# A hybrid decoder block on one core: x and the first two weight units in 256 KB pieces, transposes one piece ahead, high passes first, positions later

## Chip, cores and metric

The kernel runs on one core of a Trainium2 chip. The time is device time of the whole program in microseconds (us), the median of several runs. The profile is of one execution, whose own time stands beside its span, from the first to the last instruction.

## The reference, cut to what matters

One decoder block on 256 tokens of width 1024, in float32. An input projection feeds two groups of heads (a gated linear attention and a block attention), their outputs go through an output projection, and a gated feed-forward network follows.

```python
h = rms_norm(x, norm1_gain[l])
proj = h @ w_in[l]                       # 1024 x 3600
gq, gk, gv, gr, g_low, mq, mk, mv = ...  # slices of proj
gate_logit = (g_low @ w_gate_up[l] + b_gate[l])
log_a = jax.nn.log_sigmoid(gate_logit) / GLA_GATE_TAU
# o_gla from gq, gk, gv, gr, log_a; o_moba from rotary(mq, positions), rotary(mk, positions), mv
x = x + jnp.concatenate([o_gla, o_moba], axis=-1) @ w_out[l]
h = rms_norm(x, norm2_gain[l])
x = x + (jax.nn.silu(h @ w_ffn_gate[l]) * (h @ w_ffn_up[l])) @ w_ffn_down[l]
return rms_norm(x, final_norm_gain)
```

## The kernel before, in words

**Products in three passes.** Every float32 product is made of three matmuls of a rounded type: high part of the activations by high part of the weights (line 433), high by low (434), low by high (435). So each weight is split before use: ScalarE copies `raw` to `w_hi` (`split`, line 782), VectorE subtracts to get `w_lo` (line 997). The activations of the first projection are x transposed, multiplied by the norm gain and split in the same way: ScalarE writes `aT_hi` (line 805), VectorE `aT_lo` (line 1001). The factor of the norm, one number per token (`rstd`), is put in when a result is taken out of PSUM.

**Units and buffers.** Weights come in units of 1 MB (2048 columns per partition): `w_in` is units 0 to 11, two units (row blocks 0 to 3 and 4 to 7) for each of six blocks of 512 columns. `raw` has three slots (`RAW`), `w_hi` and `w_lo` six (`RING`). A slot of `raw` is loaded again when the low part of the unit in it is made (`raw_free`). All loads of x and the weights are issued by the SyncE queue, in the order of the code: x as two tiles of 128 tokens (512 KB each, line 278), unit 0 in two halves (line 311), the narrow columns of the gate (`low_raw`, 64 KB in pieces of 64 bytes, line 313), units 1 and 2 (line 282), six small tensors, then unit 3 and on as slots come free. GpSimd issues two small loads of its own, positions and frequencies (lines 369 and 370), before it builds the identity matrix `ident` (371, 372) that the transposes need.

**The start.** TensorE waits for `ident`, transposes the gains (449), runs four warm-up transposes (455), transposes x, tile by tile, 16 transposes (462), runs eight more warm-up transposes and then `first_unit`: for each of four row blocks k it waits for `aT_hi`, `aT_lo`, `w_hi`, `w_lo` of that row block and issues its six matmuls. We call these six a row. Unit 0 is rows 0 to 3, unit 1 rows 4 to 7. Between them come `gate_low` (16 matmuls, lines 495 and 496, whose left operand is `low_w`, split by ScalarE at 821 and GpSimd at 407) and the transposes of the other gains (483). After unit 1 come the logits (529), then units 2 to 11, with small steps between or inside them: `cumulate` (538, 540) in the middle of unit 3 needs the logarithms of the gate from VectorE (1059); `moba_transposed(1)` (522) in the middle of unit 7 needs the second rotated operand from VectorE (1081).

**The queues of the other engines.** Each engine works strictly in the order written. VectorE: activations and weights of rows 0 to 3 in turn, activations 4 to 7, unit 1, the take-out of `gate_low` (1025) and of the gains (1027), units 2 and 3, the scaled logits (1034), the angles of the rotation with the end of the gate in the middle (1059), units 4 and 5, the gate's factors on queries and keys (1086 to 1091), units 6 and 7, the first rotation, unit 8, and so on. ScalarE: activations and weights in pairs, the narrow columns (821), unit 1, the sums of squares of x (788), units 2 and 3, the take-out of block 0 (799), the gate's functions (831 to 833), units 4 and 5, the exponentials of the cumulated gate (839 to 841, which wait for `cumulate`), unit 6, sine and cosine, unit 7, the take-out of block 1, and on. GpSimd: the two loads, `ident`, the masks, the low part of the narrow columns (407), `rstd` (402, 403).

Of the kernel before, what the change touches and what calls it, by code (L numbers as in the profile page):

```python
# [22 lines left out]
P = 128  # L23
SEQ, D = 256, 1024
T = SEQ // P
# [20 lines left out]
IN_UNITS, OUT_UNITS = 2 * len(BLOCKS), 4  # L46
PHASE0 = IN_UNITS + OUT_UNITS
# [29 lines left out]
def fill(u):  # L77

    return u // RAW + (1 if u % RAW else 0)


def build_block(nc, x, positions, norm1_gain, w_in, w_gate_up, b_gate, gla_out_gain, moba_out_gain,
# [6 lines left out]
    with ExitStack() as ctx:  # L89
# [18 lines left out]

        ident = sb("ident", [P])
# [73 lines left out]
        x_loaded = [sem(f"x_loaded_{t}") for t in range(T)]  # L183
# [4 lines left out]
        first_loaded = [sem(f"first_loaded_{n}") for n in range(2)]  # L188
# [87 lines left out]
        def _(sp):  # L276
            for t in range(T):
                sp.dma_start(x_sb[:, t, :], x[0, t * P:(t + 1) * P, :]).then_inc(x_loaded[t], 16)
# [35 lines left out]
            for u in range(1, RAW):  # L314
                rows_unit(u, w_in[0], (u % 2) * 4 * P, 4, BLOCKS[u // 2], 512)
# [43 lines left out]
        def _(pool):  # L359
# [40 lines left out]
            def wide_rstd(norm, t):  # L400
# [28 lines left out]
        def _(pe):  # L429
# [16 lines left out]

            pe.wait_ge(ident_built, 1)
# [4 lines left out]
            def warm_up(n):  # L452

                for _ in range(n):
# [830 lines left out]
```

## Time and profile before

| | us |
|---|---|
| median of 3 runs | 315.05 (314.77 to 315.11) |
| the profiled execution's own time | 314.29 |
| its span | 312.3 |
| start of the first matmul of a product | 9.66 |

The page is of that one execution; times in its rows count from the first instruction. Matmul and weight-load rows are modelled in their ends, so the distance between the starts of like instructions tells more than their durations. "TensorE's granted clock" is the column PEclk. In the mean it is 0.997 of full speed.

### The profile page before, as it was taken

The page shows a single profiled execution, that of the slowest core. Times are in us where ns is not written, and L with a number is a line of the kernel's source. Part 1 is how long each engine was busy: PE and PEld are TensorE (multiplying, and loading weights), DVE is VectorE, ACT ScalarE, POOL GpSimd, SP SyncE. Part 2 cuts the span into 40 slices and gives each one's busy share as a digit, 9 for nine tenths or more (in the row PEclk, how much of TensorE's full clock was granted, in tenths as well). Part 3 has the DMA queues.
Part 4 walks back from the last instruction along what each step waited for, and adds up shares of the span by engine and source line. Part 5 has one row for each costly group of instructions (what it writes and reads, how often), then busy time and mean ns, then how long its engine had stood idle before and what let it go on. Part 6 is the DMA issues. An engine that isn't in the chain of part 4 may idle for free.

```text
span 312.3 us, 3865 instructions
## 1 busy us (share of the span) xinstructions
PE 301.4 (97%) x1424; PEld 251.2 (80%) x1424; DVE 178.9 (57%) x199; ACT 153.7 (49%) x185; POOL 21.9 (7%) x44
## 2 busy tenths in 40 slices
PE   5899999999999999999999999999999999999992
PEld 5787888888888888888888888888888888888881
DVE  0888979986686247645371809082635536280434
ACT  2978897568553437361533526070807152443124
POOL 7130100000202001500000000000000000000002
PEclk9999999999999999999999999999999999999998
DMA  7986386537744303928374564729090918330003
GB/s 224 367 277 244 118 295 206 192 134 270 253 148 139 134 0 82 309 81 283 123 242 163 184 220 137 266 72 331 18 376 9 326 77 274 129 134 0 0 2 135
DMA packets 36449, 54.45 MB, mean 174 GB/s; under 512 B 2834, under 2 KB 25540, under 8 KB 36436
## 3 DMA queue, kind: packets, MB, share of 16 engines
q1 hardware_dynamic: 36356, 54.24, 51.1%
q0 software_dynamic: 64, 0.03, 0.3%
q8 instruction: 8, 0.13, 0.2%
q14 instruction: 5, 0.04, 0.0%
q10 hardware_dynamic: 16, 0.00, 0.0%
HBM read 53.23 MB, written 1.05 MB: 174 GB/s over the span
## 4 chain that ended last, share of the span: by engine, by line
PE 94%; DMA 2%; DVE 1%; ACT 1%; issue 0%; SPq 0%; POOLq 0%; POOL 0%; DVEq 0%
PE acc L433 16%; PE acc L435 15%; PE acc L434 15%; PE aux L435 13%; PE aux L433 13%; PE aux L434 13%; PE aux L522 4%; DMA raw<-in_w_in 2%; PE aux L600 1%; DVE x_sb L1188 1%; PE aux L622 1%; PE aux L582 1%; PE aux L568 1%; DVE reuse_e L1246 0%; ACT reuse_e L974 0%
## 5 line engine op out<-in xcount | busy, mean ns | idle before, releaser
L997 DVE TENSOR_TENSOR w_lo<-raw,w_hi 128x2048 fp32r<-128x2048 f32 x48 | 107.9, 2287 | 15.2 <-ACT w_hi L782 15.2
L782 ACT CAST w_hi<-raw 128x2048 fp32r<-128x2048 f32 x48 | 89.7, 1912 | 6.5 <-PE acc L435 4.6
L433 PE MATMUL aux<-w_hi,aT_hi 128*128 128x512 f32 x176 | 69.7, 396 | 0.0
L435 PE MATMUL aux<-w_hi,aT_lo 128*128 128x512 f32 x176 | 68.8, 391 | 0.0
L434 PE MATMUL aux<-w_lo,aT_hi 128*128 128x512 f32 x176 | 68.5, 389 | 0.0
L433 PE MATMUL acc<-w_hi,aT_hi 128*128 128x512 f32 x136 | 54.9, 403 | 1.1 <-DVE w_lo L1013 1.1
L435 PE MATMUL acc<-w_hi,aT_lo 128*128 128x512 f32 x136 | 53.1, 391 | 0.0
L434 PE MATMUL acc<-w_lo,aT_hi 128*128 128x512 f32 x136 | 53.0, 390 | 0.0
L1220 DVE TENSOR_TENSOR pT_lo<-aux,pT_hi 128x512 fp32r<-128x512 f32 x10 | 6.9, 692 | 70.6 <-ACT pT_hi L943 70.6
L943 ACT CAST pT_hi<-aux 128x512 fp32r<-128x512 f32 x10 | 5.9, 587 | 76.5 <-PE aux L522 76.5
L435 PEld LDWEIGHTS aux<-w_hi,aT_lo 128*128 128x128 f32 x176 | 33.0, 188 | 7.1
L434 PEld LDWEIGHTS aux<-w_lo,aT_hi 128*128 128x128 f32 x176 | 33.1, 188 | 6.6
L433 PEld LDWEIGHTS aux<-w_hi,aT_hi 128*128 128x128 f32 x176 | 33.0, 188 | 6.5
L433 PE MATMUL acc<-w_hi,pT_hi 128*128 128x512 f32 x80 | 31.2, 390 | 0.0
L435 PE MATMUL acc<-w_hi,pT_lo 128*128 128x512 f32 x80 | 31.1, 389 | 0.0
L434 PE MATMUL acc<-w_lo,pT_hi 128*128 128x512 f32 x80 | 31.1, 389 | 0.0
L433 PEld LDWEIGHTS acc<-w_hi,aT_hi 128*128 128x128 f32 x136 | 25.6, 188 | 6.6 <-issue 1.6
L435 PEld LDWEIGHTS acc<-w_hi,aT_lo 128*128 128x128 f32 x136 | 25.5, 188 | 5.5
L434 PEld LDWEIGHTS acc<-w_lo,aT_hi 128*128 128x128 f32 x136 | 25.6, 188 | 4.9
L930 ACT ACTIVATE reuse_c<-aux,rstd 128x256 f32<-128x256 f32 x22 | 10.4, 473 | 26.3 <-PE aux L435 26.2
L434 PEld LDWEIGHTS acc<-w_lo,pT_hi 128*128 128x128 f32 x80 | 15.0, 188 | 3.1
L435 PEld LDWEIGHTS acc<-w_hi,pT_lo 128*128 128x128 f32 x80 | 15.0, 188 | 3.1
(170 smaller groups left out, 237.4 us busy)
## 6 DMA issues: line engine op xcount, KB each, us to landing
raw<-in_w_in SPq DMA_DIRECT2D x24, 512.0 KB, 4.9
raw<-in_w_ffn_gate SPq DMA_DIRECT2D x22, 512.0 KB, 4.4
raw<-in_w_ffn_up SPq DMA_DIRECT2D x22, 512.0 KB, 5.5
raw<-in_w_ffn_down SPq DMA_DIRECT2D x22, 512.0 KB, 5.8
raw<-in_w_out SPq DMA_DIRECT2D x8, 512.0 KB, 4.0
x_sb<-in_x SPq DMA_DIRECT2D x2, 512.0 KB, 3.8
out<-reuse_e SPq DMA_DIRECT2D x4, 256.0 KB, 2.4
reuse_a<-in_final_norm_gain SPq DMA_DIRECT2D x1, 512.0 KB, 4.7
```

Of the source, the lines that this page charges most:

```text
L433: nc.tensor.matmul(dst, left_hi[:, k, tok], right_hi, start=first, stop=False)
L434: nc.tensor.matmul(dst, left_hi[:, k, tok], right_lo, start=False, stop=False)
L435: return nc.tensor.matmul(dst, left_lo[:, k, tok], right_hi, start=False, stop=last)
L522: last = nc.tensor.transpose(aux[:, bank, n * P:(n + 1) * P], src, ident[:, :])
L568: last = nc.tensor.matmul(aux[:, bank, pair * SEQ:(pair + 1) * SEQ], kiT[:, pair, tok], qdT[:, pair, :, tok], start=True, stop=True)
L582: last = nc.tensor.matmul(aux[:, 2 + h // 2, (h % 2) * SEQ:(h % 2 + 1) * SEQ], mT[:, 0, h, P:SEQ], mT[:, 1, h, :], start=True, stop=True)
L600: last = nc.tensor.matmul(aux[:, bank, h * DV:(h + 1) * DV], probT[:, t + k, h, :], mv[:, k, h * DV:(h + 1) * DV], start=k == 0, stop=k == t)
L782: nc.scalar.copy(w_hi[:, slot % RING, :], raw[:, slot % RAW, :]).then_inc(hi_ready, 1)
L930: nc.scalar.activation(silu_g[:, t, :], aux[:, GATE_UP_BANKS[parity][t], 0:FF], ACT.Silu, scale=rstd[:, 1, t:t + 1]).then_inc(silu_ready, 1)
L943: nc.scalar.copy(dst, aux[:, 1, :].rearrange("p (k s) -> p k s", k=2)).then_inc(hiddenT_hi_ready, 1)
L997: nc.vector.tensor_tensor(w_lo[:, slot % RING, :], raw[:, slot % RAW, :], w_hi[:, slot % RING, :].bitcast(f32), ALU.subtract).then_inc(lo_ ...
L1220: nc.vector.tensor_tensor(lo, aux[:, 1, :].rearrange("p (k s) -> p k s", k=2), hi.bitcast(f32), ALU.subtract).then_inc(hiddenT_lo_ready, 1)
```

## The change

It does the following.

- x is loaded in four pieces of 256 columns for all 256 tokens (256 KB, contiguous pieces of 1 KB) and units 0 and 1 in eight pieces of one row block (256 KB, pieces of 2 KB), in the order x0, w0, w1, x1, w2, w3, x2, w4, w5, x3, w6, w7. The narrow columns and unit 2 follow, then the small tensors.
- TensorE begins with seven ordinary float32 matmuls of 64 columns on a tile of zeros that VectorE sets at its start, does the gains, seven more, then the four transposes of x piece 0, two more warm-up matmuls, row 0, and so on, the transposes of a piece one piece ahead of the rows. Rows 0 to 6 come before `gate_low` and the other gains, row 7 and the logits after.
- Within a row the order is both high by high matmuls, both high by low, both low by high, with a wait ahead of each pair for just what it needs.
- The high part of weight row 0 is made by VectorE; ScalarE makes those of rows 1 to 7, in an order of weights, weights, activations. VectorE subtracts in the same order. Units are counted from 2 in the semaphores of the splits.
- GpSimd issues the loads of positions and frequencies after the low part of the narrow columns.

```diff
-            for t in range(T):
-                sp.dma_start(x_sb[:, t, :], x[0, t * P:(t + 1) * P, :]).then_inc(x_loaded[t], 16)
+            def x_part(p):
+                cols = slice(p * 2 * P, (p + 1) * 2 * P)
+                sp.dma_start(x_sb[:, :, cols], x[0, :, cols].rearrange("(t p) n -> p t n", p=P)).then_inc(x_loaded[p], 16)
+
+            def first_part(n):
+                sp.dma_start(raw[:, n // 4, (n % 4) * 512:(n % 4 + 1) * 512],
+                             w_in[0, n * P:(n + 1) * P, BLOCKS[0]:BLOCKS[0] + 512]).then_inc(first_loaded[n], 16)
+
+            for p in range(X_PARTS):
+                x_part(p)
+                for n in (2 * p, 2 * p + 1):
+                    first_part(n)
...
             def raw_free(u):
 
-                if isinstance(u, int) and u == RAW:
-                    sp.wait_ge(first_lo_ready, 4)
+                if isinstance(u, int) and u < RAW + EARLY:
+                    sp.wait_ge(first_lo_ready, 4 * (u - RAW + 1))
                 else:
-                    sp.wait_ge(lo_ready, u - RAW)
-            buf = raw[:, 0, :].rearrange("p (k n) -> p k n", k=4)
-            for h in range(2):
-                sp.dma_start(buf[:, 2 * h:2 * h + 2, :], w_in[0, 2 * h * P:2 * (h + 1) * P, BLOCKS[0]:BLOCKS[0] + 512]
-                             .rearrange("(k p) n -> p k n", p=P)).then_inc(first_loaded[h], 16)
+                    sp.wait_ge(lo_ready, u - RAW - EARLY + 1)
+
             sp.dma_start(low_raw[:, :, :], w_in[0, :, LOW:LOW + RANK].rearrange("(k p) n -> p k n", p=P)).then_inc(low_loaded, 16)
-            for u in range(1, RAW):
+            for u in range(EARLY, RAW):
                 rows_unit(u, w_in[0], (u % 2) * 4 * P, 4, BLOCKS[u // 2], 512)
...
-            with nc.allow_non_contiguous_dma(reason="256 positions, one per partition and tile"):
-                pool.dma_start(pos_i[:, :], positions.rearrange("b (t p) -> p (b t)", p=P)).then_inc(pos_loaded, 16)
-            pool.dma_start(freq[:, :], inv_freq.to_broadcast([P, HALF])).then_inc(pos_loaded, 16)
             then(nc.gpsimd.memset(ident[:, :], 0.0))
             nc.gpsimd.affine_select(out=ident[:, :], in_=ident[:, :], compare_op=ALU.not_equal, fill=1.0, base=0,
                                     pattern=[[-1, P]], channel_multiplier=1).then_inc(ident_built, 1)
...
             pool.wait_ge(low_hi_ready, 1)
             nc.gpsimd.tensor_tensor(low_w[:, :, :, 1, :], low_raw[:, :, :].unsqueeze(2).to_broadcast(LOW_COPIES),
                                     low_w[:, :, :, 0, :].bitcast(f32), ALU.subtract).then_inc(low_lo_ready, 1)
+            with nc.allow_non_contiguous_dma(reason="256 positions, one per partition and tile"):
+                pool.dma_start(pos_i[:, :], positions.rearrange("b (t p) -> p (b t)", p=P)).then_inc(pos_loaded, 16)
+            pool.dma_start(freq[:, :], inv_freq.to_broadcast([P, HALF])).then_inc(pos_loaded, 16)
             for t in range(T):
                 wide_rstd(0, t)
...
-                pe.wait_ge(hi_ready, u)
-                pe.wait_ge(lo_ready, u)
+                pe.wait_ge(hi_ready, u - EARLY + 1)
+                pe.wait_ge(lo_ready, u - EARLY + 1)
...
+            def warm_up(n):
+
+                for _ in range(n):
+                    nc.tensor.matmul(acc[:, 2, 0:P // 2], warm[:, :], warm[:, 0:P // 2], start=True, stop=True)
+
+            pe.wait_ge(warm_built, 1)
+            warm_up(7)
             pe.wait_ge(ident_built, 1)
             pe.wait_ge(norm1_loaded, 16)
             nc.tensor.transpose(acc[:, 3, NORM1_ROW:NORM1_ROW + KC], gain_rows[0:KC, :],
                                 ident[0:KC, 0:KC]).then_inc(gains_in_psum, 1)
...
-            def warm_up(n):
-
-                for _ in range(n):
-                    nc.tensor.transpose(acc[:, 2, 0:P], ident[:, :], ident[:, :])
-
-            warm_up(4)
-            for t in range(T):
-                pe.wait_ge(x_loaded[t], 16)
-                for bank in range(4):
-                    for k in (2 * bank, 2 * bank + 1):
-                        last = nc.tensor.transpose(aux[:, bank, (k % 2) * SEQ + t * P:(k % 2) * SEQ + (t + 1) * P],
+            warm_up(7)
+
+            def x_transposed(part):
+
+                pe.wait_ge(x_loaded[part], 16)
+                for k in (2 * part, 2 * part + 1):
+                    for t in range(T):
+                        last = nc.tensor.transpose(aux[:, part, (k % 2) * SEQ + t * P:(k % 2) * SEQ + (t + 1) * P],
                                                    x_sb[:, t, k * P:(k + 1) * P], ident[:, :])
-                    if t == T - 1:
-                        last.then_inc(xT_in_psum, 1)
-
-            warm_up(8)
-
-            def first_unit():
-
-                for k in range(4):
-                    pe.wait_ge(xT_hi_ready, k + 1)
-                    pe.wait_ge(xT_lo_ready, k + 1)
-                    pe.wait_ge(first_hi_ready, k + 1)
-                    pe.wait_ge(first_lo_ready, k + 1)
-                    for t in range(T):
-                        last = product(acc[:, t, :], k, t, *weights(0, 512, k), k == 0, False)
-                last.then_inc(unit_used, 1)
+                last.then_inc(xT_in_psum, 1)
+
+            def first_row(k):
+
+                right_hi, right_lo = weights(k // 4, 512, k % 4)
+                toks = [slice(t * P, (t + 1) * P) for t in range(T)]
+                pe.wait_ge(xT_hi_ready, k + 1)
+                pe.wait_ge(first_hi_ready, k) if k else pe.wait_ge(row0_hi_ready, 1)
+                for t in range(T):
+                    nc.tensor.matmul(acc[:, t, :], aT_hi[:, k, toks[t]], right_hi, start=k == 0, stop=False)
+                pe.wait_ge(first_lo_ready, k + 1)
+                for t in range(T):
+                    nc.tensor.matmul(acc[:, t, :], aT_hi[:, k, toks[t]], right_lo, start=False, stop=False)
+                pe.wait_ge(xT_lo_ready, k + 1)
+                for t in range(T):
+                    last = nc.tensor.matmul(acc[:, t, :], aT_lo[:, k, toks[t]], right_hi, start=False, stop=k == KC - 1)
+                    if k == KC - 1 and t == 0:
+                        last.then_inc(tile0_in_psum, 1)
+                if k % 4 == 3:
+                    last.then_inc(unit_used, 1)
...
-                     7: [moba_scores], 9: [moba_outputs]}
-            for u in range(IN_UNITS):
-                if u == 0:
-                    first_unit()
-                else:
-                    in_unit(u, midway.get(u, ()))
+            after = {4: [gla_transposed], 6: [gla_scores], 7: [moba_scores], 9: [moba_outputs]}
+            x_transposed(0)
+            warm_up(2)
+            first_row(0)
+            x_transposed(1)
+            first_row(1)
+            x_transposed(2)
+            first_row(2)
+            first_row(3)
+            x_transposed(3)
+            for k in range(4, 7):
+                first_row(k)
+            gate_low()
+            other_gains()
+            first_row(7)
+            logits()
+            for u in range(EARLY, IN_UNITS):
+                in_unit(u, midway.get(u, ()))
                 for step in after.get(u, ()):
                     step()
...
+            def split_first(n):
+                act.wait_ge(first_loaded[n], 16)
+                cols = slice((n % 4) * 512, (n % 4 + 1) * 512)
+                nc.scalar.copy(w_hi[:, n // 4, cols], raw[:, n // 4, cols]).then_inc(first_hi_ready, 1)
 
 
             act.wait_ge(gains_ready, 1)
             take_xT((0, 1))
-            split_first(0)
-            take_xT((2, 3))
-            split_first(1)
-            take_xT((4, 5, 6, 7))
+            for p in range(1, X_PARTS):
+                split_first(2 * p - 1)
+                split_first(2 * p)
+                take_xT((2 * p, 2 * p + 1))
+            split_first(7)
             act.wait_ge(low_loaded, 16)
             nc.scalar.copy(low_w[:, :, :, 0, :], low_raw[:, :, :].unsqueeze(2).to_broadcast(LOW_COPIES)).then_inc(low_hi_ready, 1)
-            split(1)
+            split(2)
             for t in range(T):
-                act.wait_ge(x_loaded[t], 16)
                 sum_squares(0, t)
-            split(2)
             split(3)
             take_block(0, gqk)
...
-            def split_first(k):
-                dve.wait_ge(first_hi_ready, k + 1)
-                cols = slice(k * 512, (k + 1) * 512)
-                nc.vector.tensor_tensor(w_lo[:, 0, cols], raw[:, 0, cols], w_hi[:, 0, cols].bitcast(f32),
+            def split_first(n):
+                slot, cols = n // 4, slice((n % 4) * 512, (n % 4 + 1) * 512)
+                if n:
+                    dve.wait_ge(first_hi_ready, n)
+                else:
+                    dve.wait_ge(first_loaded[0], 16)
+                    nc.vector.tensor_copy(w_hi[:, 0, cols], raw[:, 0, cols]).then_inc(row0_hi_ready, 1)
+                    dve.wait_ge(row0_hi_ready, 1)
+                nc.vector.tensor_tensor(w_lo[:, slot, cols], raw[:, slot, cols], w_hi[:, slot, cols].bitcast(f32),
                                         ALU.subtract).then_inc(first_lo_ready, 1)
 
+            nc.vector.memset(warm[:, :], 0.0).then_inc(warm_built, 1)
             dve.wait_ge(gains_in_psum, 1)
             nc.vector.tensor_copy(gains[:, 0:KC], acc[:, 3, 0:KC]).then_inc(gains_ready, 1)
             dve.wait_ge(gains_ready, 1)
-            for k in range(4):
-                take_xT((k,))
-                split_first(k)
-            take_xT((4, 5, 6, 7))
-            split(1)
+            split_first(0)
+            take_xT((0, 1))
+            for p in range(1, X_PARTS):
+                split_first(2 * p - 1)
+                split_first(2 * p)
+                take_xT((2 * p, 2 * p + 1))
+            split_first(7)
             dve.wait_ge(low_in_psum, 1)
```

## Rows read from the trace of the kernel before

**Rows 1.** The page, part 1: busy us of each engine.

```profile
PE 301.4 (97%) x1424; PEld 251.2 (80%) x1424; DVE 178.9 (57%) x199; ACT 153.7 (49%) x185; POOL 21.9 (7%) x44
```

**Rows 2.** The chain that ended last, in order of time: start, us, what.

```profile
1.71 6.44 DMA raw<-in_w_in
...
24.22 0.43 PE acc L433
...
32.61 0.86 PE aux L538 x4
...
59.96 0.87 PE aux L522 x8
...
302.15 0.70 DVE x_sb L1188
```

**Rows 3.** Stretches: us, busy of each engine, granted clock, DMA share, GB/s.

```profile
5.50:6.50 1.00, 1.00 (x7) 1.00 (x6) 0.00 (x0) 0.00 (x0) 0.93 (x6) 1.00 0.93 185
10.00:11.00 1.00, 1.00 (x6) 0.83 (x5) 1.00 (x3) 1.00 (x4) 0.00 (x0) 1.00 1.04 383
```

**Rows 4.** GpSimd's queue, 4 to 8 us (packets, MB, share); landings of x, `in_w_ffn_gate`.

```profile
q0 software_dynamic: 63, 0.03, 20.1%
...
DMA to landing us min/median/max: 3.4/3.8/4.3
...
DMA to landing us min/median/max: 3.9/4.4/6.2
```

**Rows 5.** Timeline of GpSimd at the start: start, us, engine, line, operation.

```profile
1.32 0.93 POOL L369 DMA_DIRECT2D pos_i<-in_positions  x1 [0.82 <-POOLq L1275]
2.25 0.58 POOL L370 DMA_DIRECT2D freq<-in_inv_freq  x1
```

**Rows 6.** Timeline of TensorE, 3.6 to 17.4 us.

```profile
3.63 0.27 PE L449 MATMUL acc<-ident,reuse_d 8*128 8x8 f32 x1 [3.63 <-POOL ident L372]
...
5.59 0.63 PE L462 MATMUL aux<-ident,x_sb 128*128 128x128 f32 x2
...
7.02 0.49 PE L462 MATMUL aux<-ident,x_sb 128*128 128x128 f32 x3
...
9.66 0.47 PE L433 MATMUL acc<-w_hi,aT_hi 128*128 128x512 f32 x1 [1.06 <-DVE w_lo L1013]
...
15.19 0.28 PE L495 MATMUL acc<-aT_hi,w_hi 128*128 128x256 f32 x1
...
16.98 0.28 PE L496 MATMUL acc<-aT_lo,w_hi 128*128 128x256 f32 x1
```

**Rows 7.** Weight loads by line: count, ns min/median/max, starts.

```profile
L449 PEld LDWEIGHTS acc<-ident,reuse_d x1: 178/178/178, 3.6 to 3.6; 8*128 8x128 f32 x1
...
L483 PEld LDWEIGHTS acc<-ident,reuse_d x1: 132/132/132, 17.2 to 17.2; 10*128 10x128 f32 x1
...
L600 PEld LDWEIGHTS aux<-mv,reuse_f x24: 188/192/192, 78.1 to 80.7; 128*128 128x128 f32 x24
```

**Rows 8.** Timeline of ScalarE.

```profile
7.17 0.84 ACT L805 ACTIVATE aT_hi<-aux,gains 128x256 fp32r<-128x256 f32 x2 [4.47 <-PE aux L462]
8.17 1.14 ACT L811 CAST w_hi<-raw 128x512 fp32r<-128x512 f32 x2 [0.16 <-DMA raw<-in_w_in]
...
34.38 0.60 ACT L839 ACTIVATE reuse_c<-aux 128x512 f32<-128x512 f32 x1 [0.84 <-PE aux L540]
```

**Rows 9.** Timeline of VectorE.

```profile
17.30 0.41 DVE L1025 COPY lowT<-acc 32x256 f32<-32x256 f32 x1
...
18.88 4.49 DVE L997 TENSOR_TENSOR w_lo<-raw,w_hi 128x2048 fp32r<-128x2048 f32 x2 [1.09 <-ACT w_hi L782]
24.26 0.88 DVE L1034 SCALAR_TENSOR_TENSOR reuse_b<-aux,rstd,mv 128x256 f32<-128x256 f32 x2 [0.89 <-PE aux L529]
...
30.08 0.69 DVE L1059 SCALAR_TENSOR_TENSOR reuse_b<-reuse_b 128x512 f32<-128x512 f32 x1
...
58.46 0.69 DVE L1081 TENSOR_TENSOR reuse_e<-reuse_e,mv 128x512 f32<-128x512 f32 x1
```

More of the change, by code:

```diff
@@ L46 @@
 IN_UNITS, OUT_UNITS = 2 * len(BLOCKS), 4
+EARLY = 2
+X_PARTS = 4
 PHASE0 = IN_UNITS + OUT_UNITS
@@ L77, in fill @@
 def fill(u):
-    return u // RAW + (1 if u % RAW else 0)
+    return u // RAW + (1 if u % RAW >= EARLY else 0)
 def build_block(nc, x, positions, norm1_gain, w_in, w_gate_up, b_gate, gla_out_gain, moba_out_gain,
@@ L107, in build_block @@
         pT_lo = sb("pT_lo", [2, SEQ], f32r)
+        warm = sb("warm", [P])
         ident = sb("ident", [P])
@@ L180, in build_block @@
         ang, turns, turns_lo, sin_arg = (reuse_e[:, n * T * HALF:(n + 1) * T * HALF] for n in range(4))
-        x_loaded = [sem(f"x_loaded_{t}") for t in range(T)]
+        x_loaded = [sem(f"x_loaded_{p}") for p in range(X_PARTS)]
         rows_loaded = sem("rows_loaded")
@@ L187, in build_block @@
         bias_loaded = sem("bias_loaded")
-        first_loaded = [sem(f"first_loaded_{n}") for n in range(2)]
+        first_loaded = [sem(f"first_loaded_{n}") for n in range(4 * EARLY)]
+        warm_built = sem("warm_built")
+        row0_hi_ready = sem("row0_hi_ready")
         up_loaded = sem("up_loaded")
@@ L708, in _ @@
                       9: [probs_transposed], 10: [gla_updates], 11: [lambda: heads_transposed(0, (3, 0)), gla_outputs]}
-            after = {0: [gate_low, other_gains], 1: [logits], 4: [gla_transposed], 6: [gla_scores],
-                     7: [moba_scores], 9: [moba_outputs]}
-            for u in range(IN_UNITS):
-                if u == 0:
-                    first_unit()
-                else:
-                    in_unit(u, midway.get(u, ()))
+            after = {4: [gla_transposed], 6: [gla_scores], 7: [moba_scores], 9: [moba_outputs]}
[16 more added lines that the diff above has]
+                in_unit(u, midway.get(u, ()))
                 for step in after.get(u, ()):
@@ L806, in take_xT @@
                                   gains[:, NORM1_ROW + k:NORM1_ROW + k + 1]).then_inc(xT_hi_ready, 1)
-            def split_first(half):
-                act.wait_ge(first_loaded[half], 16)
-                for k in (2 * half, 2 * half + 1):
-                    nc.scalar.copy(w_hi[:, 0, k * 512:(k + 1) * 512], raw[:, 0, k * 512:(k + 1) * 512]).then_inc(first_hi_ready, 1)
+            def split_first(n):
+                act.wait_ge(first_loaded[n], 16)
+                cols = slice((n % 4) * 512, (n % 4 + 1) * 512)
+                nc.scalar.copy(w_hi[:, n // 4, cols], raw[:, n // 4, cols]).then_inc(first_hi_ready, 1)
             act.wait_ge(gains_ready, 1)
             take_xT((0, 1))
-            split_first(0)
-            take_xT((2, 3))
-            split_first(1)
-            take_xT((4, 5, 6, 7))
+            for p in range(1, X_PARTS):
[3 more added lines that the diff above has]
+            split_first(7)
             act.wait_ge(low_loaded, 16)
             nc.scalar.copy(low_w[:, :, :, 0, :], low_raw[:, :, :].unsqueeze(2).to_broadcast(LOW_COPIES)).then_inc(low_hi_ready, 1)
-            split(1)
+            split(2)
             for t in range(T):
-                act.wait_ge(x_loaded[t], 16)
                 sum_squares(0, t)
-            split(2)
             split(3)
@@ L951, in ffn_phase @@
                 for n in range(n_units):
-                    split_as(slot + 3 + n, fills - (0 if (slot + n) % RAW else 1), u + (n + 4 - RING))
+                    split_as(slot + 3 + n, fills + (1 if (slot + n) % RAW >= EARLY else 0), u + (n + 4 - RING))
                 take_gate(j, u, parity)
@@ L995, in split @@
                 slot = u if slot is None else slot
-                dve.wait_ge(hi_ready, u)
+                dve.wait_ge(hi_ready, u - EARLY + 1)
                 nc.vector.tensor_tensor(w_lo[:, slot % RING, :], raw[:, slot % RAW, :],
```

## The prediction

> **What bounds the kernel now.** First the page's busy times: TensorE works 301.4 of 312.3 us [rows 1], so the time is TensorE's order plus what lies before and after it. The chain that ended last says where it is not TensorE: it starts with the load of the first weights, landing at 1.71 + 6.44 = 8.15, reaches TensorE's products at 9.66 and leaves them at 302.15 [rows 2, 6]. Between these TensorE has no wait worth naming, so a gain at the start reaches the end only if every later wait has room for it. So the third reading is the timelines of the other engines: how much earlier could TensorE come to each step before its input is the late one? Two places are tight. `cumulate` starts at 32.61 and its input, from VectorE's line 1059, is ready at 30.08 + 0.69 = 30.77: room 1.84. `moba_transposed(1)` starts at 59.96, its input is ready at 58.46 + 0.69 = 59.15: room 0.81 [rows 2, 9].
>
> **The loads.** In 5.50 to 6.50 the DMA engines moved 185 GB/s, at 10 to 11 us 383 [rows 3]; GpSimd's two small loads took 20% of the engines' time in 4 to 8 us for 0.03 MB [rows 4]. Issued later, they leave that room to x and the weights. At 383 GB/s a 256 KB piece takes 0.68 us. The x tiles (pieces of 4 KB, 512 KB each) took 3.4 and 4.3 us from issue to landing; the quickest load in pieces of 1 KB, also 512 KB, 3.9 [rows 4]. Half of it is 0.7 less: x0, issued at 0.8, lands at about 4.0. One piece lands per 0.68 us after it: w0 4.7, x1 6.0, x2 8.1, x3 10.1, w7 11.5, with the narrow columns behind at 12.5 and unit 2 at 15. SyncE issues 12 loads in place of 4, at some 0.4 us each, quicker than they move. What waits on w0 to w7 and x0 to x3 is costed below; landings by this list come before each use.
>
> **The moved loads' other side.** GpSimd spends 0.93 + 0.58 issuing them [rows 5], now behind the low part of the narrow columns and ahead of `rstd`; both `rstd` and positions are then needed only after 24 us, some 3 and 1.5 us after I have them ready. `ident`, for which TensorE waited to 3.63 [rows 6], comes those 1.5 us earlier, at 2.1.
>
> **The warm-up.** VectorE's memset lets TensorE start at about 1.05. Seven float32 matmuls are 14 matmul instructions: an ordinary float32 matmul shows as two. What does one of 64 columns cost, with its weight load of 128 columns? The trace has none. Its bounds: the transposes of 128 columns are 0.21 apart at the start (two in 0.63, less the 0.42 of the last), so 64 columns are 0.107, nothing less; at most a slow weight load. A transpose's weight load takes 178 ns before the clock rises and 132 after [rows 7]: 46 ns that scale and 86 that don't. An ordinary one takes 188 at the quick clock, so 102 scale, and 204 ns at the slow one. I take 0.21, the nearer to these rows. At the quick clock it is 0.107 either way. TensorE's page in the Trainium skill, "TensorE: Matmul & The Clock Gate", LDWEIGHTS, gives columns by 1.2 GHz, 107 ns for 128 columns with no word on the clock gate; by it the warm-up would cost 1.5 us each time, which is the second case below. No row here shows it at the slow clock.
>
> When does the clock rise? PEclk says 1.00 from the first microsecond, but the starts tell otherwise: equal transposes stand 0.21 apart at 5.6 us and 0.11 (0.49 less 0.27, halved) at 7.0 [rows 6]; 1.2 and 2.4 GHz. The change of step lies at 6.7, 3.1 us after TensorE's first work at 3.63. I take the same after its new start, some 4.3. So: first seven 1.05 to 4.0; gains to 4.2; second seven, nearly all quick, to 5.8; the four transposes of x0, landed long since, 0.45 to 6.25; two warm-up matmuls to 6.7, in the shadow of ScalarE's first `aT_hi` (7.17 for two took 0.84 [rows 8], so 0.42 each: 6.35 to 6.8). The first weight row is ready by then (copy and subtract, 0.7 each, from 4.7). **Row 0 starts at S = 6.8 instead of 9.66.**
>
> **The rows.** 24 matmuls of unit 0 took 9.66 to 15.19, so a row is 1.38 [rows 6]. Does anyone keep TensorE waiting once it runs? ScalarE does two weight rows (0.57 each) and two activations (0.42) per pair, 2.0 us; VectorE some 0.65 for a weight row (a quarter of half of 4.49 [rows 9], and its fixed part) and as much as ScalarE for the activations, 2.2 us; TensorE's pair with its transposes takes 3.2. Walked through from S: row 0 has its last pair at S + 0.9, its `aT_lo` at S + 0.85; every later row finds its inputs 0.3 us or more early, with x1 and x2 landed. So the dense stretch begins at S. High passes first are what makes row 0 start on `w_hi` and `aT_hi` alone; if all four inputs had to be there it would cost 0.85.
>
> Before the take-out of `gate_low` there now stand seven rows, three groups of transposes and 16 matmuls (15.19 to 16.98 and the next, 1.9 [rows 6]): 9.7 + 1.35 + 1.9 + 0.1 = 13.05. So VectorE takes out at S + 13.05 = 19.85, where before it did at 17.30 [rows 9]. **This is the step that eats the gain:** VectorE waits for it, idle from about 16, and units 2 and 3 are queued behind. Take-outs 0.5, then 4.49 for both units: unit 2 is ready at 22.65, unit 3 at 24.85, and the scaled logits begin at 24.9. Before: 24.26. VectorE is 0.6 later.
>
> TensorE itself would be through row 7 (21.4) and the logits (about 1 us) at 22.5, and starts unit 2 at 22.7, when it is ready, against 24.22 [rows 2]: 1.5 ahead. `cumulate` it would reach at 31.1, but its input comes at 30.77 + 0.6 = 31.4: 1.15 ahead is left. ScalarE had waited 0.84 for `cumulate` before 34.38 [rows 8]; it comes 0.6 later itself, so the exponentials start 0.2 earlier, and its chain on to the rotation, through VectorE, ends 0.2 earlier: 58.95. TensorE, at 58.8, goes on at 59.0: 0.95 ahead. After it VectorE and ScalarE wait for TensorE again at each step, so that passes to the end. In one formula, near here: gain = 7.8 - S.
>
> **The sum:** span 312.3 - 1.0 = 311.3, and with the 2.0 around it 313.3 for the profiled execution's 314.29. The median stands 0.76 above that execution: 314.0.
>
> **Rivals.**
> - *A weight load is not slowed by the slow clock.* Then each warm-up burst takes 1.5: 1.05 to 2.55, the gains when they have landed, the second to 4.4, transposes still partly slow to 5.1; S = 5.6, bounded below by x0 and `aT_hi` at 5.3. Gain 2.2 to 2.5: 312.7. For it: nothing but the low bound, 0.107. Against it: the 178 beside 132.
> - *The clock rises late, and it ends slower.* If it rises no sooner than before, at 6.7, because short loads count as little work or the gains interrupt them, the second burst lasts to 6.9, transposes to 7.4, S = 7.95: +0.2 us. If it is still slow when the rows start, S is 8.5 and each slow matmul of a row costs 0.21 more; with a rise some 1 us later the dense stretch is as if from 9.1: +1.3, 316.3. It decides from S = 7.8 on. For it: the warm-up is 28 short instructions in front of transposes whose x has landed at 4.0. The same skill page, in its section on the clock gate, says the slow state is the default and activity releases it; the transposes of this trace agree.
> - *Pieces of 256 KB move slowly.* The skill's "DMA: Bandwidth & Descriptors", Bandwidth, advises 1 MiB for 75% of the peak. As a mechanism here: at the 185 GB/s of 5.5 to 6.5 [rows 3] in place of 383, twelve pieces land by 19, unit 2 by 25.5 and TensorE waits there some 5 us, about 317 to 320. Against it: many loads are in flight at once, and 383 was reached with 512 KB ones behind one another.
> - *Nothing changes:* the two warm-up bursts and `gate_low`'s later place together take what the earlier rows give, S between 7.2 and 8.4.
>
> **How the numbers follow.** Forecast as walked (S 6.3 to 7.3) 0.44; quick weight loads 0.22; late clock 0.18; slow pieces or another queue late 0.06; no change 0.10. About 0.2% (0.6 us) is what a measurement of this kernel can tell. Faster by more: all of the second case and most of the first, 0.61. Within: the fourth, a part of the first and of the late clock, 0.21. Slower: 0.18. The range goes from the quick weight loads, 312.5, to the late clock's middle, 315.8; the forecast alone is 313.5 to 314.5.
>
> **What would show it.** First products at 6.8; starts of equal instructions halving at about 4.3; the 14 warm-up instructions 0.21 apart before it; no wait between rows 0 and 6; the `gate_low` take-out at 19.9 with VectorE idle before it; short waits of TensorE before unit 2, at `cumulate` and at `moba_transposed(1)`. Wrong if S is above 7.8, if rows wait for pieces of x or weights, or if the waits in the middle are not there and the whole 2.9 us comes through.

## The result and the profile after

The changed kernel took a median of 317.45 us (316.86 to 317.62, four runs) beside 314.91 for the kernel before (314.67 to 315.11, four runs): ratio 1.0079, 95% interval 1.0067 to 1.0091. The forecast was 314.0 in a range of 312.5 to 315.8, so it missed in size and in sign. The profiled execution took 317.62 with a span of 315.6.

The page of the changed kernel, part 1, busy time of each engine; the engines other than TensorE do what they did [rows 1], and TensorE has 20 instructions and 6.6 us more:

```profile
PE 308.0 (98%) x1444; PEld 256.7 (81%) x1444; DVE 179.5 (57%) x204; ACT 153.3 (49%) x187; POOL 21.2 (7%) x44
```

The timeline of TensorE at its start, changed kernel (start, us, engine, line, operation, names, shapes, count, wait before it):

```profile
1.12 3.25 PE L461 MATMUL acc<-warm 128*128 128x64 f32 x14 [1.12 <-DVE warm L1051]
4.29 0.27 PE L467 MATMUL acc<-ident,reuse_d 8*128 8x8 f32 x1
4.50 3.25 PE L461 MATMUL acc<-warm 128*128 128x64 f32 x14
7.54 1.06 PE L477 MATMUL aux<-ident,x_sb 128*128 128x128 f32 x4
8.39 0.95 PE L461 MATMUL acc<-warm 128*128 128x64 f32 x4
9.23 1.22 PE L488 MATMUL acc<-w_hi,aT_hi 128*128 128x512 f32 x2
...
12.58 0.71 PE L488 MATMUL acc<-w_hi,aT_hi 128*128 128x512 f32 x2
```

The two bursts follow each other at the same pace: the second, forecast nearly all quick, takes 3.25 like the first, 0.21 from start to start inside a burst. Nothing behind it waits by the timeline, so row 0 starts at 9.23, hardly sooner than the 9.66 of before [rows 6]. Its weights have long been there; its `aT_hi`, made from the slow transposes, is ready at 9.12 (ScalarE starts at 8.70 and takes 0.84 for two).

The chain that ended last, changed kernel, in order of time, tells when the pace turns:

```profile
9.34 1.11 PE acc L488 x2
10.45 0.85 PE acc L491 x2
11.30 0.85 PE acc L494 x2
12.16 0.67 PE aux L477 x4
12.82 0.47 PE acc L488 x2
13.29 0.47 PE acc L491 x2
```

Two products of 512 columns take 0.85 until 12.2 and 0.45 to 0.47 from 12.8 on: 1.2 and 2.4 GHz. From row 0 to row 1 the changed kernel takes from 9.23 to 12.58, 3.35 us; in the first experiment below, quick from row 0 on, it is 7.53 to 9.39, 1.86. In the terms of the forecast's formula that is a dense stretch begun at 9.23 + 1.49 = 10.7, and 7.8 - 10.7 = -2.9; the spans differ by 3.3, the medians by 2.5.

Stretches of the changed kernel (us; busy of PE, PEld, DVE, ACT, POOL; granted clock, DMA share, GB/s):

```profile
5.50:6.50 1.00, 1.00 (x7) 1.00 (x6) 0.46 (x1) 0.00 (x0) 0.48 (x3) 1.00 0.99 258
7.50:8.50 1.00, 1.00 (x8) 1.00 (x7) 0.00 (x0) 0.00 (x0) 0.00 (x0) 1.00 1.08 399
9.30:12.20 2.90, 2.90 (x9) 2.22 (x9) 2.08 (x4) 1.26 (x3) 0.00 (x0) 1.00 1.14 343
12.60:15.60 3.00, 3.00 (x17) 2.51 (x16) 1.87 (x4) 2.74 (x7) 0.00 (x0) 1.00 0.94 327
```

The granted clock says 1.00 in both of the last two, though 9 instructions fit into 2.90 us of the one and 17 into 3.00 of the other. At the start of this kernel only the starts of equal instructions tell the clock. The DMA engines moved 258 GB/s where before they moved 185 [rows 3], and no row waits for a load. The landings of x, same kernel, in us from issue:

```profile
DMA to landing us min/median/max: 2.8/5.2/6.2
```

The first x piece, issued at 0.80, is there at 3.6; the later ones, at 7.1, 9.2 and 11.4, came some 1.2 later than forecast, still before their use here.

VectorE in the changed kernel, its timeline:

```profile
23.92 0.41 DVE L1063 COPY lowT<-acc 32x256 f32<-32x256 f32 x1 [3.68 <-PE acc L516]
...
24.34 4.47 DVE L1027 TENSOR_TENSOR w_lo<-raw,w_hi 128x2048 fp32r<-128x2048 f32 x2
28.74 0.86 DVE L1072 SCALAR_TENSOR_TENSOR reuse_b<-aux,rstd,mv 128x256 f32<-128x256 f32 x2
...
34.53 0.69 DVE L1097 SCALAR_TENSOR_TENSOR reuse_b<-reuse_b 128x512 f32<-128x512 f32 x1
```

Before, the take-out was at 17.30 and the scaled logits at 24.26 [rows 9]; now 23.92, after 3.68 of idleness, and 28.74. TensorE meets it at both of the tight places, and each comes some three microseconds later (timeline of TensorE, changed kernel; before 32.45 and 59.80 in this view, 32.61 and 59.96 in the chain [rows 2]):

```profile
35.28 1.13 PE L558 MATMUL aux<-reuse_b,tri_mid 128*128 128x256 f32 x4
...
62.92 1.09 PE L542 MATMUL aux<-ident,reuse_e 128*128 128x128 f32 x8
```

Their inputs are ready just ahead of them: at 34.53 + 0.69 = 35.22 by the line of VectorE above, and at 62.87 in the chain, which from 23.9 to there runs over VectorE and the engines that feed it.

### The profile page after: what moved, and what is told of

It reads as the page before. It is cut to its first block, busy times and chain, and to the rows that moved or that the text cites. A ratio compares the mean times of both kernels' runs of the same rounds, so it can differ in the third digit from the quotient of the medians.

```text
span 315.6 us, 3917 instructions
## 1 busy us (share of the span) xinstructions
PE 308.0 (98%) x1444; PEld 256.7 (81%) x1444; DVE 179.5 (57%) x204; ACT 153.3 (49%) x187; POOL 21.2 (7%) x44
## 4 chain that ended last, share of the span: by engine, by line
PE 84%; DVE 10%; issue 2%; DMA 2%; ACT 1%; POOLq 0%; SPq 0%; POOL 0%; DVEq 0%
PE aux L446 13%; PE aux L444 13%; PE aux L445 13%; PE acc L446 11%; PE acc L444 11%; PE acc L445 11%; PE aux L542 3%; DVE w_lo L1027 3%; PE acc L461 2%; DMA raw<-in_w_in 2%; DVE reuse_e L1088 1%; PE acc L488 1%; PE acc L491 1%; PE acc L494 1%; PE aux L620 1%
## 5 line engine op out<-in xcount | busy, mean ns | idle before, releaser
L1027 DVE TENSOR_TENSOR w_lo<-raw,w_hi 128x2048 fp32r<-128x2048 f32 x47 | 105.6, 2286 | 12.5 <-ACT w_hi L813 12.5
L813 ACT CAST w_hi<-raw 128x2048 fp32r<-128x2048 f32 x47 | 87.8, 1912 | 8.2 <-PE acc L446 4.6
L444 PE MATMUL acc<-w_hi,aT_hi 128*128 128x512 f32 x120 | 48.5, 404 | 0.0
L446 PE MATMUL acc<-w_hi,aT_lo 128*128 128x512 f32 x120 | 46.9, 391 | 0.0
L445 PE MATMUL acc<-w_lo,aT_hi 128*128 128x512 f32 x120 | 46.8, 390 | 0.0
L446 PEld LDWEIGHTS acc<-w_hi,aT_lo 128*128 128x128 f32 x120 | 22.5, 188 | 4.8
L444 PEld LDWEIGHTS acc<-w_hi,aT_hi 128*128 128x128 f32 x120 | 22.6, 188 | 4.7 <-issue 0.4
L445 PEld LDWEIGHTS acc<-w_lo,aT_hi 128*128 128x128 f32 x120 | 22.6, 188 | 4.4
```

What stands on the lines that cost most here:

```text
L444: nc.tensor.matmul(dst, left_hi[:, k, tok], right_hi, start=first, stop=False)
L445: nc.tensor.matmul(dst, left_hi[:, k, tok], right_lo, start=False, stop=False)
L446: return nc.tensor.matmul(dst, left_lo[:, k, tok], right_hi, start=False, stop=last)
L813: nc.scalar.copy(w_hi[:, slot % RING, :], raw[:, slot % RAW, :]).then_inc(hi_ready, 1)
L1027: nc.vector.tensor_tensor(w_lo[:, slot % RING, :], raw[:, slot % RAW, :], w_hi[:, slot % RING, :].bitcast(f32), ALU.subtract).then_inc(lo_ ...
```

## The experiments

Each ratio is to the kernel before on the same chip. Three groups of four ran, each on a chip of its own; times are compared directly only inside a group, unless the text says otherwise. A ratio need not be the quotient of the two medians to the last digit. "S" is the start of row 0's first products in the timeline.

### First group: what leaves the clock slow, and what the parts do alone (kernel before: 314.70)

**Warm-up of 128 columns.** The forecast had priced a narrow matmul but not asked whether it does what a wide one does. Below, theory A is that it is the narrow matmuls that leave the clock slow, theory B that it is the zeros, theory C that it is neither.

```diff
-                    nc.tensor.matmul(acc[:, 2, 0:P // 2], warm[:, :], warm[:, 0:P // 2], start=True, stop=True)
+                    nc.tensor.matmul(acc[:, 2, 0:P], warm[:, :], warm[:, :], start=True, stop=True)
```

> The changed kernel with warm-up matmuls of 128 columns in place of 64; the tile stays zero, the counts too. [...] Then 128 columns, at the same 0.22 us each, raise it at some 4.3 us, row 0 starts at about 7.0 at the quick clock, and the time is some 4 us below the changed kernel's 317.45, about 1 below before's. Theory B, zeros: a tile of zeros raises no clock whatever its width; then nothing changes, 317.5. Theory C, the clock rises at a moment that doesn't hang on this work: no change either.

Measured: 314.79, ratio 1.000 (0.998 to 1.002). TensorE's timeline, warm-up of 128 columns:

```profile
1.12 3.36 PE L461 MATMUL acc<-warm 128*128 128x128 f32 x14 [1.12 <-DVE warm L1051]
...
4.60 1.86 PE L461 MATMUL acc<-warm 128*128 128x128 f32 x14
6.30 0.60 PE L477 MATMUL aux<-ident,x_sb 128*128 128x128 f32 x4
6.74 0.61 PE L461 MATMUL acc<-warm 128*128 128x128 f32 x4
7.53 0.73 PE L488 MATMUL acc<-w_hi,aT_hi 128*128 128x512 f32 x2 [0.18 <-ACT aT_hi L836]
...
9.39 0.70 PE L488 MATMUL acc<-w_hi,aT_hi 128*128 128x512 f32 x2
```

The first burst takes as long as the narrow one, so width costs nothing at the slow clock; the second takes 1.86 in place of 3.25, because the pace turns early in it, and row 0 is quick from its first product. Without the narrow matmuls the whole slowdown is gone. Of the 4 us that theory A forecast, 2.7 came: row 0 starts at 7.53 and not at 7.0, and by the formula 7.8 - 7.53 = 0.3 is left against the kernel before, which this measurement can't tell from nothing.

**Warm-up of ones,** 64 columns. Rival: it is the zeros that leave the clock slow.

```diff
-            then(nc.vector.memset(warm[:, :], 0.0))
+            then(nc.vector.memset(warm[:, :], 1.0))
```

> The changed kernel with the warm-up tile set to ones in place of zeros, 64 columns as they were. Theory A (narrow warm-up): no change, 317.5, the clock rises near 12.5 us. Theory B (zeros): it rises at some 4.3 us and the time falls by about 4 us.

Measured: 317.59, ratio 1.0083 (1.006 to 1.0105). Its timeline of TensorE repeats the changed kernel's rows to within a hundredth as far as row 0's start at 9.23 and turns quick at some 11.0. It is 2.80 slower than the 128 columns on the same chip, so the values explain none of the loss.

**No warm-up at all.** All three calls of `warm_up` are taken out, the rest as changed.

> The changed kernel without any warm-up matmul. If they only delay, as theory A says of the 64-column ones, row 0 starts when x piece 0 has landed and is transposed and its high part made, at about 5.5 us in place of 9.34, at the slow clock; with 3.1 us of dense work before the rise it turns quick at some 8.7, and the time is 3 to 4 us below the changed kernel's, some 313.5 to 314.5. If the warm-up helps at all (theory C with a rise at 12.5 in any case) rows stay slow to 12.5 and the time falls by about 2 us only.

Measured: 314.57, ratio 0.9986 (0.9965 to 1.0007). From the chain that ended last, without warm-up:

```profile
0.80 3.24 DMA x_sb<-in_x
4.08 1.13 PE aux L475 x4
5.30 0.48 ACT aT_hi L833
5.83 1.22 PE acc L486 x2
...
20.09 0.57 POOL rstd L411
21.02 4.66 POOL rstd L411
```

The time is just above the forecast's range. Row 0 starts at 5.83, slow, and the pace turns at some 9.7, a microsecond later than forecast. So the changed kernel's warm-up is worse than none: its two bursts hold TensorE to 7.54 while x landed at 3.6, the clock rises later than without it, and the run with ones, equal to it in time, is 3.0 slower on this chip. Against two bursts of 128 columns (314.79) no warm-up at all can't be told apart.

GpSimd's second power took 4.66 in the chain, eight times the 0.57 of the first, and held the scaled logits to 26.19. The timelines of GpSimd and VectorE show with what it coincides, first without warm-up, then in the kernel before:

```profile
21.02 5.08 POOL L411 TENSOR_TENSOR rstd<-ms,minus_half 128x1 f32<-128x1 f32 x1
21.21 4.47 DVE L1024 TENSOR_TENSOR w_lo<-raw,w_hi 128x2048 fp32r<-128x2048 f32 x2
```

```profile
15.00 2.29 DVE L997 TENSOR_TENSOR w_lo<-raw,w_hi 128x2048 fp32r<-128x2048 f32 x1 [0.93 <-ACT w_hi L782]
16.11 1.23 POOL L402 TENSOR_SCALAR ms<-ss 128x1 f32<-128x1 f32 x1 [1.61 <-ACT reuse_f L788]
```

The chain's piece ends at 25.68, where VectorE's subtractions of units 2 and 3 end. In the kernel before `ms` ends at 17.34, the subtraction at 17.29, and the next `ms`, with none beside it, takes 0.19. Up to 26 us each of the seven `ms` and `rstd` instructions that start inside such a subtraction, in six traces, lasts until it ends or longer; those with none beside them take 0.2 and 0.57. So the subtraction seems to hold them up, though no run tests that alone. In the run without warm-up the power starts 0.19 before the subtraction; in the first experiment one that starts 0.21 before takes 0.55.

**The positions' loads alone moved,** in the kernel before, to the place where the change has them.

> The kernel before with only the two loads of positions and frequencies moved behind the low part of the narrow columns. ident comes 1.5 us earlier, at 2.1; the first weights land up to 0.8 us earlier, and row 0, which waits for their low part at 9.66, starts 0.3 to 0.8 us earlier; of that 0.3 to 0.8 reaches the end: 314.1 to 314.6. The rival: the transposes of x and the clock set the start, and nothing moves.

Measured: 314.39, ratio 0.9991 (0.9968 to 1.0015): no difference. The stretch and the chain of that kernel:

```profile
5.50:6.50 1.00, 1.00 (x6) 1.00 (x5) 0.00 (x0) 0.00 (x0) 0.23 (x1) 1.00 0.95 299
```

```profile
1.71 6.71 DMA raw<-in_w_in
...
9.94 0.47 PE acc L433
```

And TensorE's timeline, positions moved:

```profile
4.13 3.68 PE L462 MATMUL aux<-ident,x_sb 128*128 128x128 f32 x16 [0.52 <-DMA x_sb<-in_x]
7.60 1.40 PE L455 MATMUL acc<-ident 128*128 128x128 f32 x8
```

Without the small packets the engines move 299 GB/s instead of 185 [rows 3], but the load that row 0 waits for lands at 8.42, not before the 8.15 of [rows 2]. The room went to other transfers. This run also bears on the step that failed: TensorE's first work moved from 3.63 to 2.32, with a pause before x, yet all 16 transposes of x (3.47 from the first start to the next line) stand 0.21 apart, and the pace turns only at 8.3, where in the kernel before it had turned at some 6.9. The rise did not come earlier with an earlier start even with the kernel's own instructions of 128 columns. The forecast's reading of the 20% in [rows 4] as time that the weights would get was wrong, though nothing hung on it.

### Second group: the step that eats the gain, and the waits (kernel before: 314.75)

All four have the warm-up of 128 columns.

**Unit 2 ahead of the take-out.** VectorE idles before `gate_low`'s take-out while unit 2 lies ready for it.

```diff
             split_first(7)
+            split(2)
             dve.wait_ge(low_in_psum, 1)
...
-            split(2)
             split(3)
```

> The changed kernel with 128-column warm-ups, and VectorE makes unit 2's low part before it waits for the take-out of gate_low, in its 3.7 us of idle time there. My account says that VectorE's scaled logits then start at some 23.3 in place of 25.5, unit 2 no longer waits, TensorE starts it at 23.4, 0.8 ahead of before, and nothing in the middle holds it: 313.9 where the same kernel without this edit gave 314.8 and before 314.7. Rival: gate_low's later place costs nothing, the early start alone is what is small; then no change against 314.8.

Measured: 314.10, ratio 0.9972 (0.9956 to 0.9988), near the forecast. TensorE and VectorE, unit 2 first:

```profile
25.27 0.87 DVE L1072 SCALAR_TENSOR_TENSOR reuse_b<-aux,rstd,mv 128x256 f32<-128x256 f32 x2
59.88 1.04 PE L542 MATMUL aux<-ident,reuse_e 128*128 128x128 f32 x8
```

Row 0 started at 8.29 in this execution, so the scaled logits begin 17.0 after it, where the old order has 18.0, and TensorE waits at neither tight place. The same kernel without the edit (third group, last run) has row 0 at 8.28, waits 0.17 at `cumulate`, starts `moba_transposed(1)` at 60.52 and ends with a span of 313.2 instead of 312.4. So VectorE's idle time was worth some 0.6 to 0.8 us; the two ratios, from two chips, just touch. The way was in part another than forecast: unit 2 starts 15.9 after row 0 with the edit and 16.0 without, and the scaled logits come 1.2 later after row 0 than forecast, because VectorE waited 1.06 for ScalarE's high part of unit 3.

**The same with one burst,** the `warm_up(7)` after the gains taken out.

> The last kernel without the second burst of seven warm-up matmuls; the first seven end at 4.4, x piece 0 has landed at 3.6. Expected: transposes at 4.6 to 5.1 or 5.4, row 0 at 5.8 to 6.1 in place of 7.5, the clock up at 4.7; the 1.5 us pass through to the end as far as VectorE lets them: 312.4 to 312.8. Rival: the work is broken off and the clock rises late, at 8 or more; then some 313.5 to 314.

Measured: 313.31, ratio 0.9956 (0.9944 to 0.9969). VectorE's timeline, unit 2 first and one burst:

```profile
18.37 2.29 DVE L1026 TENSOR_TENSOR w_lo<-raw,w_hi 128x2048 fp32r<-128x2048 f32 x1 [2.43 <-ACT w_hi L812]
20.58 0.40 DVE L1063 COPY lowT<-acc 32x256 f32<-32x256 f32 x1
22.25 2.29 DVE L1026 TENSOR_TENSOR w_lo<-raw,w_hi 128x2048 fp32r<-128x2048 f32 x1 [1.19 <-ACT w_hi L812]
24.46 0.87 DVE L1071 SCALAR_TENSOR_TENSOR reuse_b<-aux,rstd,mv 128x256 f32<-128x256 f32 x2
```

Row 0 started at 6.34, and the gain is 1.4 us; the time is 0.5 above the forecast's range. Here the new order no longer makes VectorE earlier: it waits 2.43 for ScalarE's high part of unit 2, the take-out waits for that work, and the scaled logits begin 18.1 after row 0, as in the old order (18.0 in the first experiment). TensorE waits 0.20 at `cumulate`.

**All waits ahead of each row,** instead of each ahead of its own pass.

```diff
                 pe.wait_ge(first_hi_ready, k) if k else pe.wait_ge(row0_hi_ready, 1)
+                pe.wait_ge(first_lo_ready, k + 1)
+                pe.wait_ge(xT_lo_ready, k + 1)
                 for t in range(T):
                     nc.tensor.matmul(acc[:, t, :], aT_hi[:, k, toks[t]], right_hi, start=k == 0, stop=False)
-                pe.wait_ge(first_lo_ready, k + 1)
...
-                pe.wait_ge(xT_lo_ready, k + 1)
```

> 128-column warm-ups, and a row waits for all four of its inputs before its first matmul; the order of the matmuls stays. By my account only row 0 is late by it, 0.4 to 0.85 us (its low activations come 0.9 after its high ones), later rows have their inputs; the time is that much above the 314.8 of the same kernel with waits pair by pair: 315.2 to 315.7. Rival: later rows are held too, then 1.5 and more.

Measured: 315.59, ratio 1.0032 (1.002 to 1.0044). TensorE's timeline, all waits first:

```profile
8.82 0.70 PE L490 MATMUL acc<-w_hi,aT_hi 128*128 128x512 f32 x2 [1.16 <-DVE aT_lo L1031]
```

Only row 0 is held, by 1.16; no later row waits. Of this 0.18 is there with the waits pair by pair too (first experiment), and the next run, whose pace turned at the same 5.4, has row 0 at 7.83: high passes first are worth 1.0 here, and the forecast's price for it was 0.85.

**Positions first,** the two small loads back at GpSimd's start.

> 128-column warm-ups, positions and frequencies issued at GpSimd's start as in before. ident comes 1.5 us later, but the first burst lasts to 4.4 anyway, and pieces land up to 0.8 us later, none of which is late for its row: no change against 314.8. Rival: the small packets hold x piece 0 or the first weights, and row 0 starts up to 0.5 us later.

Measured: 315.31, ratio 1.0019 (1.001 to 1.0027), row 0 at 7.83. Against 1.000 (0.998 to 1.002) and 0.9997 (0.9984 to 1.001) for the same kernel without it, on other chips, the intervals touch. Whether the two loads cost 0.2% or nothing can't be told from it.

### Third group: the best version, and the two clocks on one chip (kernel before: 314.57)

**One burst, VectorE's order as changed,** 128 columns.

> 128-column warm-ups, only the first burst of seven, VectorE's order as in the changed kernel (unit 2 after the take-out). Row 0 as in the run with unit 2 first and one burst, 6.3, take-out at 19.6, both units by 24.5, scaled logits at 24.6 where that run had 24.5: so within 0.3 us of that run's 313.3. Rival: VectorE's idle time matters at any start; then some 1 us worse, 314.3.

Measured: 313.91, ratio 0.9972 (0.996 to 0.9984), row 0 at 6.13 and quick; 0.6 above the run it was to equal. The formula gives 1.7 less than before; 0.7 came by the medians, 0.9 by the ratio. Pieces 1 and 2 of x landed at 7.78 and 9.88 and held their transposes 0.2 each. And the chain went through GpSimd: `ms` 1.90 from 20.70, then `rstd` 2.06 from 22.68, both beside VectorE's subtractions of units 2 and 3 (20.27 to 24.74), after which the scaled logits began at 25.25, and TensorE waited 0.74 at `cumulate`. On this chip one burst is 0.73 faster than two (314.64, last run); with unit 2 first it was 0.79 (313.31 against 314.10).

**A burst of five and unit 2 first:** one burst, shorter by two matmuls.

> One burst of five 128-column matmuls, unit 2 first on VectorE. The burst ends at 3.4, transposes of x piece 0 from 3.6, row 0 at 5.3 to 5.6, one us earlier than with seven. If the clock still rises between 5 and 7, rows 0 and 1 are partly slow, and VectorE waits for unit 2, landing at 16.4: so 0 to 0.4 us below 313.3. Rival: with less work before it the clock rises later and the time is 0.5 above.

Measured: 313.01, ratio 0.994 (0.9926 to 0.9955), the fastest of all. TensorE's timeline, burst of five:

```profile
1.11 2.50 PE L461 MATMUL acc<-warm 128*128 128x128 f32 x10 [1.11 <-DVE warm L1050]
...
4.30 1.12 PE L476 MATMUL aux<-ident,x_sb 128*128 128x128 f32 x4 [0.48 <-DMA x_sb<-in_x]
5.21 1.06 PE L461 MATMUL acc<-warm 128*128 128x128 f32 x4
6.04 1.22 PE L487 MATMUL acc<-w_hi,aT_hi 128*128 128x512 f32 x2
...
8.77 0.69 PE L476 MATMUL aux<-ident,x_sb 128*128 128x128 f32 x4
```

The time is within the forecast, but not by its way: in the profiled execution row 0 is slow and the pace turns only at 8.9, and yet this kernel wins by 1.56 us in the median. TensorE begins x when x lands, and a slow row costs 1.3 once (6.04 to 9.22 for a row and its transposes, instead of 1.86). That execution, at 313.42, is the slowest of the six; where the pace turned in the others isn't known. Against the burst of seven (0.9956, 0.9944 to 0.9969, other chip) it can't be told apart.

**The changed kernel again,** and **the warm-up of 128 columns again**.

> The changed kernel itself, to have it on the same chip as the next one: 2.5 to 3 us above before.

> The changed kernel with 128-column warm-ups once more, beside the changed kernel on the same chip: 2.5 to 3 us below it, within 0.5 us of before. Where its second burst turns quick varies from execution to execution, between 4.7 and 6.5 us.

Measured: 317.31, ratio 1.0084 (1.0068 to 1.01), and 314.64, ratio 0.9997 (0.9984 to 1.001). On one chip 2.67 us separate two kernels that differ in the columns of 16 matmul calls. The second burst of the changed kernel takes 3.25 again, and this is the timeline of TensorE with 128 columns:

```profile
4.60 2.61 PE L461 MATMUL acc<-warm 128*128 128x128 f32 x14
```

This time the pace turned at some 6.3 within the second burst, not at 4.9 as in the first experiment: equal kernels differ in the moment.

## Why the prediction was wrong, point by point

- **The step that failed:** "I take the same after its new start, some 4.3", the moment of the clock's rise. It took the 3.1 us between the first work and the rise in the kernel before, whose instructions were of 128 columns, and carried it to 28 of 64 columns. Measured: 12.5 in the changed kernel, 11.2 in its repeat and 11.0 with ones; 4.9 to 6.5 with 128 columns and a first burst of seven. That the width makes the difference is shown by changing it alone, on one chip (2.67 us), and on another against the narrow kernel with ones (2.80). The carrying over was unsound beyond the width: with the positions moved, the kernel before starts 1.3 earlier and its pace turns 1.4 later. The reading of the kernel before was off by little: single starts put its step at some 6.9, not 6.7. Likewise 31.4 at `cumulate` leaves 1.2 and not 1.15, and nothing hangs on either.
- **S.** Forecast 6.8, measured 9.23. Of the 2.4 between, the second burst, "nearly all quick", took 3.25 and ended 1.7 late, and transposes and last two warm-ups, slow as well, made up the rest. With the clock risen early enough S was 7.53, 0.7 late: the rise came at some 4.9 instead of 4.3, the second burst started at 4.60, not 4.2, and from the transposes to row 0 it was 1.23 instead of 1.0.
- **A narrow warm-up matmul.** Forecast 0.21 between its bounds; measured 0.21. Narrow and wide ones stand equally far apart at the slow clock, so the rival of quick weight loads is out. The loads' own records last 0.33 there, where its split into a part that scales and one that doesn't gives 0.29. For a weight load the Trainium skill gives the columns divided by 1.2 ("TensorE: Matmul & The Clock Gate", LDWEIGHTS), by estimate 107 ns for 128 columns. The trace does not agree at the slow clock, where even matmuls of 64 columns stand 0.21 apart.
- **The late-clock rival** had the right mechanism and too small a size. It was priced with a rise some 1 us into the rows, a dense stretch "as if from 9.1", 316.3. In the profiled execution it came some 3 us into them (9.3 to 12.5), so the stretch is as if from 10.7. Of its two reasons the gains between the bursts are out, since the wide kernel has them too. Its short loads are the same in both kernels; what the experiments show is that the 64 columns of the matmuls make the rise late. Its chance of 0.18 rested on a rise "no sooner than before", and it stopped there instead of asking how late it could be.
- **The take-out at S + 13.05:** 20.73 - 7.53 = 13.20 with 128 columns, 23.92 - 10.7 = 13.2 in the changed kernel. Right, and so is VectorE's idle time before it. The scaled logits at S + 18.1: 18.0.
- **gain = 7.8 - S:** -2.9 for 10.7 (spans -3.3, medians -2.5: the profiled execution of the kernel before was 0.6 quicker than its median, that of the changed kernel 0.2 slower). With 128 columns 0.3 for 7.53 and -0.5 for 8.28, measured -0.1 both times, with 0.6 and 0.4 either way, so these neither bear it out nor contradict it. For 6.34 it gives 1.5, measured 1.4; that kernel has unit 2 first, which the formula doesn't contain, but its scaled logits came 18.1 after row 0 all the same. One burst alone, 1.7 against 0.7, is a miss: two pieces of x were 0.2 late each, and `rstd` of GpSimd, "needed only after 24 us, some 3 and 1.5 us after", was the late input, long beside VectorE's subtraction.
- **Loads:** first piece and first weights on time (3.6 and 4.5 for 4.0 and 4.7), later ones some 1.2 late, all hidden in the changed kernel, but not with one burst alone. Pieces of 256 KB were not slow: 399 GB/s. The positions' move by itself gave nothing that its run could tell. Of the short waits forecast for TensorE, those at `cumulate` and `moba_transposed(1)` are there, and with unit 2 first the profiled executions show 0.6 to 0.8 us less; the one before unit 2 is next to nothing.

What stays open is what in a 64-column matmul fails to raise the clock, and what spreads the rise of kernels with equal first instructions over 4.9 to 6.5. Widths between, or a narrow matmul with fewer weight loads, were not tried.

## What to carry to other kernels

A warm-up is there to change a state, so before its microseconds are counted, ask whether its instructions are like those that changed the state in the trace: here the same calls at 128 columns cost the same time and saved 2.7 us. Let it end when the first real input lands: a warm-up that holds back real work loses what it earns, and in this kernel one burst of seven beat two of seven on two chips, by 0.7 and 0.8 us. Compare it with none, too. That any warm-up gains here isn't shown: with the same order on VectorE none gave 0.9986 (0.9965 to 1.0007) and one burst 0.9972 (0.996 to 0.9984), on two chips, and none with unit 2 first was not run. Where one work's input moves later (`gate_low`), put ready work of the waiting engine ahead of the wait.

## What was not expected of the hardware

- Matmuls of 64 columns behind weight loads of 128 run no quicker than those of 128 at the slow clock (both 0.21 apart), and 28 of them, from 1.1 to 7.5 us, left TensorE slow, where bursts of 10 to 28 of 128 columns were followed by a rise at 4.9 to 8.9. With no warm-up it came at 9.7; with narrow ones at 11.0 to 12.5.
- The granted clock of the stretches reads 1.00 while starts of equal instructions are 0.43 apart instead of 0.23.
- GpSimd's small loads took 20% of the DMA engines' time; without them the rate rose from 185 to 299 GB/s and the awaited load landed at 8.42 instead of 8.15.
- Two short instructions of GpSimd, over one element for each partition, took 0.2 and 0.57 alone, and up to 1.9 and 5.1 beside VectorE's subtraction of a unit, at whose end or 0.4 later they ended. In two kernels that held the chain.
